# Feed-forwards with the two parts of x side by side: one 512-wide matmul for the weights' high part

## The reference

```python
h = rms_norm(x, norm_ffn_g[i])
x = x + swiglu(h, ffn_w_gate_up[i], ffn_w_down[i])      # first block
x = x + rms_norm_2(swiglu_2(h, w_gate, w_up, w_down), norm_ffn_post[layer])   # second block

def swiglu_2(h, w_gate, w_up, w_down):
    return (jax.nn.silu(h @ w_gate) * (h @ w_up)) @ w_down
```

## Time and profile before

| | us |
|---|---|
| three runs, median (range) | 2918.84 (2915.59 to 2919.42) |
| the profiled execution | 2916.95 |
| its span, first to last instruction | 2915.2 |
| TensorE busy with matmuls | 2592.3 (89%) |
| VectorE, ScalarE, GpSimd busy | 1676.4, 1193.9, 533.6 |

### The profile page before, as it was taken

How to read it: one execution, slowest core, us unless ns; L and a number is a source line. 1 busy time by engine, 2 the same in 40 slices (tenths; PEclk the granted TensorE clock), 3 DMA queues, 4 the chain that set the end, 5 groups by cost and what they waited for, 6 DMA issues and landing times. The chain is left out here.

```text
span 2915.2 us, 49758 instructions
## 1 busy us (share of the span) xinstructions
PE 2592.3 (89%) x19384; PEld 2465.6 (85%) x19390; DVE 1676.4 (58%) x2753; ACT 1193.9 (41%) x1927; POOL 533.6 (18%) x410
## 2 busy tenths in 40 slices
PE   7999898997889888999899975789988999988998
PEld 6999787997788677999799974489987999988998
DVE  3778794666555444566466675346656454334665
ACT  2534563444444323444244452234444344334443
POOL 1110692000455000000000022000002555440000
PEclk9999799999899888999899986589998999988999
DMA  4465003454334521455155532034541212103452
GB/s 158 153 207 192 16 2 112 156 182 146 99 130 155 159 33 28 143 187 189 65 173 173 167 129 73 17 116 142 182 153 58 66 59 73 66 30 116 137 183 97
DMA packets 107152, 344.26 MB, mean 118 GB/s; under 512 B 20432, under 2 KB 26160, under 8 KB 106480
## 3 DMA queue, kind: packets, MB, share of 16 engines
q1 hardware_dynamic: 106992, 342.07, 35.9%
HBM read 340.86 MB, written 1.16 MB: 117 GB/s over the span
## 5 line engine op out<-in xcount | busy, mean ns | idle before, releaser
L134 PE MATMUL ps<-h_high,hi 128*128 128x256 f32 x2936 | 851.6, 290 | 53.9 <-DVE h_low L272 38.1
L135 PE MATMUL ps<-h_low,hi 128*128 128x256 f32 x2936 | 840.6, 286 | 0.0
L136 PE MATMUL ps<-h_high,lo 128*128 128x256 f32 x2936 | 840.1, 286 | 0.0
L101 ACT ACTIVATE hi<-raw 128x1024 fp32r<-128x1024 f32 x623 | 644.7, 1052 | 439.9 <-PE ps L136 426.0
L111 DVE TENSOR_TENSOR lo<-raw,hi 128x1024 fp32r<-128x1024 f32 x521 | 629.5, 1225 | 318.7 <-ACT hi L101 318.2
L134 PEld LDWEIGHTS ps<-h_high,hi 128*128 128x128 f32 x2936 | 573.0, 195 | 62.5 <-DVE h_low L272 41.6
L135 PEld LDWEIGHTS ps<-h_low,hi 128*128 128x128 f32 x2936 | 573.2, 195 | 0.4
L136 PEld LDWEIGHTS ps<-h_high,lo 128*128 128x128 f32 x2936 | 572.9, 195 | 0.0
L111 POOL TENSOR_TENSOR lo<-raw,hi 128x1024 fp32r<-128x1024 f32 x102 | 242.6, 2383 | 491.4 <-ACT hi L101 491.3
L134 PE MATMUL ps<-hidden_h,hi 128*128 128x256 f32 x1056 | 299.3, 283 | 10.0 <-DVE lo L111 9.6
L135 PE MATMUL ps<-hidden_l,hi 128*128 128x256 f32 x1056 | 298.0, 282 | 0.0
(11 more groups left out here) (429 smaller groups left out, 4410.7 us busy)
## 6 DMA issues: line engine op xcount, KB each, us to landing
raw<-in_weights SPq DMA_DIRECT2D x623, 512.0 KB, 3.4
at_bias<-bias_group SPq DMA_DIRECT2D x64, 64.0 KB, 2.6
s_bn<-in_s_bn SPq DMA_DIRECT2D x4, 512.0 KB, 4.9
consts<-in_consts SPq DMA_DIRECT2D x1, 1794.5 KB, 9.3
x<-in_x SPq DMA_DIRECT2D x1, 1024.0 KB, 5.0
s_cT<-in_s_b SPq DMA_DIRECT2D x1, 1024.0 KB, 7.3
s_cw<-in_s_c SPq DMA_DIRECT2D x1, 1024.0 KB, 10.9
s_cT<-s_rows SPq DMA_DIRECT2D x16, 64.0 KB, 2.7
```

The source lines that it names most:

```text
L101: act.activation(k.hi[:, item % CUT, :], k.raw[:, item % RAW, :], ACT.Copy).then_inc(k.item_rounded, 1)
L134: pe.matmul(out, wh, xh, start=start, stop=False, **more)
L135: pe.matmul(out, wh, xl, start=False, stop=False, **more)
L136: return pe.matmul(out, wl, xh, start=False, stop=stop, **more)
```

## The change

Both parts of x become one tile, `both`, 128 x 2 x 8 x 256, of which `h_high` and `h_low` are views. In gate and up of every feed-forward the weight's high part multiplies both parts of x in one matmul of 512 columns into a whole bank, of which the left half takes the product with x's high part and the right half that with its low part. The weight's low part multiplies x's high part, 256 columns, into the left half. Gate and up then need a bank each: 4 and 5 for even b, 6 and 7 for odd b. ScalarE copies the right halves out, VectorE adds them to the left ones and then multiplies. As banks 6 and 7 are in use at the start, up(1) waits for the root; and layer 0's transposes go to bank 4 after down(6), with TensorE waiting for their copy. Down is as before.

```diff
+            def wide(w, bank, j):
+                wh, wl = w
+                pe.matmul(k.ps[:, bank, :], wh, k.both[:, :, j, :], start=(j == 0), stop=False)
+                return pe.matmul(k.ps[:, bank, 0:T], wl, k.both[:, 0, j, :], start=False, stop=(j == KT - 1))
 ...
                     for half in range(2):
-                        mm = product(pe, k.ps[:, 4, half * T:(half + 1) * T], w.tile(half * ITEM + j), pair_tile(src, j),
-                                     start=(j == 0 and half == 0), stop=(j == KT - 1), skip_group_check=True)
+                        mm = wide(w.tile(half * ITEM + j), 4 + half, j)
 ...
                 for half in range(2):
+                    if b == 1 and half == 1:
+                        pe.wait_ge(k.root_done.s, prep.b_root + prep.passes)
                     for j in range(KT):
-                        mm = product(pe, k.ps[:, 4 + b % 2, half * T:(half + 1) * T], w.tile((at + half) * ITEM + j),
-                                     pair_tile(src, j), start=(j == 0), stop=(j == KT - 1))
+                        mm = wide(w.tile((at + half) * ITEM + j), 4 + 2 * (b % 2) + half, j)
 ...
             # ScalarE, step b
-                act.wait_ge(k.gate_done.s, i * (2 * per) + (2 * b + b_gate + 1))
+                bank = 4 + 2 * (b % 2)
+                act.wait_ge(k.hidden_done.s, i * per + (b + b_hid - 1))
+                act.wait_ge(k.item_used, i * ROUND_ITEMS + (first + 3 * b + (2 if b == 0 else 1)))
+                act.activation(gate[:, b % 2, :], k.ps[:, bank, T:2 * T], ACT.Copy).then_inc(k.up_copied.s, 1)
+                act.wait_ge(k.item_used, i * ROUND_ITEMS + (first + 3 * b - 1))
+                act.activation(up[:, b % 2, :], k.ps[:, bank + 1, T:2 * T], ACT.Copy).then_inc(k.up_copied.s, 1)
+                act.wait_ge(k.gate_done.s, i * (4 * per) + (4 * b + b_gate + 2))
 ...
             # VectorE, step b
-                dve.tensor_tensor(gate[:, b % 2, :], k.ps[:, 4 + b % 2, 0:T], k.rs[:, 0, :], ALU.mult).then_inc(k.gate_done.s, 1)
+                dve.wait_ge(k.up_copied.s, i * (2 * per) + (2 * b + b_copied + 1))
+                dve.tensor_tensor(gate[:, b % 2, :], k.ps[:, bank, 0:T], gate[:, b % 2, :], ALU.add).then_inc(k.gate_done.s, 1)
+                dve.wait_ge(k.gate_done.s, i * (4 * per) + (4 * b + b_gate + 1))
+                dve.tensor_tensor(gate[:, b % 2, :], gate[:, b % 2, :], k.rs[:, 0, :], ALU.mult).then_inc(k.gate_done.s, 1)
 ...
-                dve.tensor_tensor(up[:, b % 2, :], k.ps[:, 4 + b % 2, T:2 * T], k.rs[:, 0, :], ALU.mult).then_inc(k.gate_done.s, 1)
-                dve.wait_ge(k.gate_done.s, i * (2 * per) + (2 * b + b_gate + 2))
+                dve.wait_ge(k.up_copied.s, i * (2 * per) + (2 * b + b_copied + 2))
+                dve.tensor_tensor(up[:, b % 2, :], k.ps[:, bank + 1, 0:T], up[:, b % 2, :], ALU.add).then_inc(k.gate_done.s, 1)
+                dve.wait_ge(k.gate_done.s, i * (4 * per) + (4 * b + b_gate + 3))
+                dve.tensor_tensor(up[:, b % 2, :], up[:, b % 2, :], k.rs[:, 0, :], ALU.mult).then_inc(k.gate_done.s, 1)
+                dve.wait_ge(k.gate_done.s, i * (4 * per) + (4 * b + b_gate + 4))
 ...
     def tensor(self, pe, b):
-        if b == 5:
+        if b == 6:
             pe.wait_ge(self.V.s, self.v0 + LAMBDA_TICK)
-            pe.transpose(self.k.ps[0:ST, 6, 0:P], self.lr, const(self.k, "ident"))
-            pe.transpose(self.k.ps[0:ST, 6, P:2 * P], self.li, const(self.k, "ident")).then_inc(self.flipped.s, 1)
+            pe.transpose(self.k.ps[0:ST, 4, 0:P], self.lr, const(self.k, "ident"))
+            pe.transpose(self.k.ps[0:ST, 4, P:2 * P], self.li, const(self.k, "ident")).then_inc(self.flipped.s, 1)
+            pe.wait_ge(self.A.s, self.a0 + 6)
 ...
-        k.hp = sb("h_high", [P, KT, T], F32R), sb("h_low", [P, KT, T], F32R)
+        k.both = sb("h_parts", [P, 2, KT, T], F32R)
+        k.hp = k.both[:, 0, :, :], k.both[:, 1, :, :]
```

More of the change, by code:

```diff
@@ L501, in swiglu @@
     rounds = (FT - 2) // per
-    b_gate, b_silu, b_hid, b_prod = k.gate_done.n, k.silu_done.n, k.hidden_done.n, k.mul_done.n
+    b_gate, b_silu, b_hid, b_prod, b_copied = k.gate_done.n, k.silu_done.n, k.hidden_done.n, k.mul_done.n, k.up_copied.n
     def walk(engine, step):
@@ L602, in step @@
                 dve.wait_ge(k.item_used, i * ROUND_ITEMS + (first + 3 * b + (2 if b == 0 else 1)))
-                dve.tensor_tensor(gate[:, b % 2, :], k.ps[:, 4 + b % 2, 0:T], k.rs[:, 0, :], ALU.mult).then_inc(k.gate_done.s, 1)
-                dve.wait_ge(k.item_used, i * ROUND_ITEMS + (first + 3 * b - 1))
-                dve.tensor_tensor(up[:, b % 2, :], k.ps[:, 4 + b % 2, T:2 * T], k.rs[:, 0, :], ALU.mult).then_inc(k.gate_done.s, 1)
-                dve.wait_ge(k.gate_done.s, i * (2 * per) + (2 * b + b_gate + 2))
+                bank = 4 + 2 * (b % 2)
+                dve.wait_ge(k.up_copied.s, i * (2 * per) + (2 * b + b_copied + 1))
+                dve.tensor_tensor(gate[:, b % 2, :], k.ps[:, bank, 0:T], gate[:, b % 2, :], ALU.add).then_inc(k.gate_done.s, 1)
+                dve.wait_ge(k.gate_done.s, i * (4 * per) + (4 * b + b_gate + 1))
+                dve.tensor_tensor(gate[:, b % 2, :], gate[:, b % 2, :], k.rs[:, 0, :], ALU.mult).then_inc(k.gate_done.s, 1)
+                dve.wait_ge(k.item_used, i * ROUND_ITEMS + (first + 3 * b - 1))
+                dve.wait_ge(k.up_copied.s, i * (2 * per) + (2 * b + b_copied + 2))
[3 more added lines that the diff above has]
+                dve.wait_ge(k.gate_done.s, i * (4 * per) + (4 * b + b_gate + 4))
                 dve.wait_ge(k.silu_done.s, i * per + (b + b_silu + 1))
@@ L626, in swiglu @@
     k.used += items
-    k.gate_done.n += 2 * FT
+    k.gate_done.n += 4 * FT
+    k.up_copied.n += 2 * FT
     k.silu_done.n += FT
@@ L824, in scalar @@
             act.wait_ge(self.flipped.s, 1)
-            act.activation(self.rows64, k.ps[0:ST, 6, 0:2 * P], ACT.Copy).then_inc(A.s, 1)
+            act.activation(self.rows64, k.ps[0:ST, 4, 0:2 * P], ACT.Copy).then_inc(A.s, 1)
     def tick(self, dve, ins):
@@ L2786, in build @@
         k.gate_done = counted("gate_and_up_scaled")
+        k.up_copied = counted("gate_and_up_low_product_copied")
         k.warm = sb("warm", [P, 1])
```

## The result

The changed kernel takes **2930.68 us** (median of 9 runs, 2925.15 to 2935.34), the kernel before beside it 2917.89 (9 runs, 2912.64 to 2922.53): ratio 1.0043 [1.0029, 1.0056], slower by 12.8 us. The prediction said 2912.2, faster or the same, with 2896 to 2926 as its range. It was wrong in sign, and the time lies outside its range.

What follows compares the result with a forecast made beforehand. TensorE, busy 89% of the span, was taken to bound the kernel. Savings of 23.0 us less costs of 16.4 gave net -6.6: 2910.3 against the profiled execution, 2912.2 us as median, with 2896 to 2926 as 8-in-10 range.

Steps and rivals of the forecast that it cites:

- The saving per tile: Gate and up: wide plus narrow matmul take 347.1 ns instead of 360, 12.9 ns saved a tile, 23.0 us in all.
- Starts: Feed-forward starts: first cut for down(0) lands 0.45 us later, 2.25 us over five loops, plus 0.5 in layer 0.
- Ends: Down(21) at five loop feed-forward ends: TensorE stalls 0.85 us each for the late hidden tile, 4.25 us in all.
- S5's rows: Layer 0, transposes moved to after down(6): rows spread and weights 4.9 us later, TensorE idle near 11.5 us.
- VectorE in layer 0: Tiles 10 to 21: added vector work makes VectorE the bound, 4.5 us more, bounds 3 and 8.
- Rival A: Wide matmul runs like the attention's `at_pl` ones: 7.7 ns a tile, 13.7 saved, 16.4 spent, +2.7: 2921.5 us; chance 0.18.
- Rival B: Wide matmul costs 240 ns, by columns' gap or two-piece operand; nothing saved: 2935.2 us; decides from 234 ns; chance 0.13.

Runs made afterwards that it cites:

- e4: Changed kernel without ScalarE's copies and VectorE's adds, all matmuls kept, x's low part computed but not added in: 2909.14 us.
- e6: Changed kernel with each gate or up item's eight wide products ahead of its eight narrow ones: wide product 230.9 ns, layers 1 to 5 feed-forwards 969.8 us.
- e1: Changed kernel with the two parts of x side by side in each feature tile, so the wide operand is one piece: 2932.55 us.
- e5: Changed kernel without the narrow product of the weights' low part in gate and up, so part of the work is left out: 229.4 ns a wide product.
- g2: g1 with set 21 of each feed-forward and sets 12 to 21 of layer 0 on the old three products, no copies or adds: 2891.66 us, ratio 0.9910.
- g1: Changed kernel with each item's eight wide products ahead of its eight narrow ones and the S5 transposes behind down(4): 2905.0 us.
- e2: Changed kernel with layer 0's transposes behind down(4) instead of down(6), their copy in ScalarE's step 4: 17.4 us less than the changed kernel.
- a_again: The changed kernel once more, unedited, for a second profile: 2931.02 us in the profiled execution.
- The pads: Runs p1, p2, q1, q2 and q3: products of zeros added ahead of the last down product of feed-forwards, as work of known price; ratios 1.0012 to 1.0053.
- p1: Kernel before with four 512-column products of zeros ahead of each feed-forward's last down product: 9.0 us over before for a price of 5.4, ratio 1.0032.
- q2: Changed kernel with eight 512-column products of zeros ahead of each feed-forward's last down product: 2934.36 us, 7.2 below its price.
- q3: e3 with four products of zeros ahead of the last down product in layers 1 to 5: 2922.38 us, 3.0 below its price.
- p2: Kernel before with eight products of zeros ahead of each feed-forward's last down product: 10.7 us over before for a price of 10.9, ratio 1.0035.
- e3: Changed kernel with wide products in layers 1 to 5 only, layer 0 and its transposes as in the kernel before: 2920.9 us.
- b1: Kernel before with only the S5 transposes moved from behind down(5) to behind down(4), their copy in ScalarE's step 4: 2905.6 us.
- q1: Changed kernel with four 512-column products of zeros ahead of each feed-forward's last down product: 2929.67 us, 6.4 below its price.

## Why the prediction was wrong

Two steps failed: the size of the saving, and the stages outside the feed-forwards, which the sum put at nothing.

**The saving per tile was about half.** I took 227.1 ns for a wide product from 512-wide products that follow one another, and measured 235.8 between narrow ones. The narrow one came at 117.1 instead of 120, together 353 for a tile (5.65 us over 16), not 347.1: 6.9 ns saved, not 12.9. Over the 1650 tiles counted for the loop feed-forwards that is 11.4 us instead of 21.3. The pitch was outside the 222 to 232 that the prediction set itself as its limit. The saving exists, with or without the copies and adds (e4). Why it is half stays open: order has a part in it (e6), the layout has none (e1), and the 5.55 us behind down(0) show the forecast pitch in the same order. By the Trainium skill, "TensorE: Matmul & The Clock Gate", section "Back-to-back issue gap", the gap of a lone 512-wide product would be 215.8 ns. Sixteen in a row without a change of width took 229.4 each here (e5), 16 above the bare 213.3 where the page's formula has 2.5.

**Starts: predicted 2.25 us slower, measured 2.1 faster.** That is the other way than the 2.25 us of the prediction's sum for them. From the first gate matmul to down(0) the five loop feed-forwards take 0.30 to 0.59 us less each: 18.43 became 18.05, 19.02 became 18.43, 18.04 became 17.74, 18.70 became 18.29 and 18.69 became 18.30. I let the table load wait for the product "as now"; but the copies bring ScalarE's table loads forward, beside the reciprocal, and that is worth more than the add costs. From the last product of zeros to down(0) it is 6.72 us in the kernel before, 6.35 after, and 6.72 again without the copies (e4).

**Ends: right.** Down(21) starts 0.89 us later at each of five ends, forecast 0.85 (the list of waits has 0.73 of it); with the slower restart the five ends cost 5.0 us, forecast 4.25. The wait is absent in e4, and g2, which does set 21 the old way, takes 193.2 for a feed-forward where g1 takes 194.0.

**S5's rows: right.** Idle 10.62 against 11.5; the two steps around the spread cost 4.3 us more, forecast 4.9. e2 removes it.

**VectorE in layer 0: right mechanism, size short.** Of the nine steps ahead of the last two downs, four take 8.77 instead of 8.50, one 9.95 and one 9.05. Against the kernel before, at 8.61 each, they cost 2.1 us, and the wait before the last down with its cold products 4.7 (1.6 of this is the clock at 0.62, which I did not price): 6.8, forecast 4.5 with 8 as its bound. Layer 0 as a whole: +10.7 (+13.3 in a_again), forecast +8.2. In mid-loop VectorE is busy 38.22 us of 50 and not 36: the 0.71 us counted distances between starts, while each of the two adds is 0.42 us of busy time. It cost nothing there.

**Outside: not in the prediction at all.** Feed-forwards: forecast -6.6, measured +2.4 (+5.3 in a_again). That alone would have given 2920 to 2923, inside the range. The rest, 6.1 us in the first profiles, 8.7 in a_again and 7.5 to 10.4 by the median, lies in stages that nobody edited and that the sum put at nothing. Their granted clock is below full (0.91 and 0.89 on average in the delta net's stage, 0.77 behind layer 3), and their cost moves when they are shifted. The two profiles cannot tell this from an effect of the change; nor could a_again. The pads show that such a move of 3 to 7 us exists (p1, q2, q3), and that the 4.5 and the 1.7 us named above also appear without wide products (p1, p2). They do not show how much of the loss it makes up, and why the kernels after, e1 and e3 lie at the dear end together was not settled.

Rival A had nearly the right saving, 7.7 ns, and its +2.7 is near the +2.4 of the feed-forwards. The second is partly luck: starts came 4.3 us better than in its sum, layer 0 and the ends worse. Rival B's deciding point, a wide matmul of 234 ns, was passed at 235.8, but neither of its mechanisms holds: e1 excludes the two pieces, and a gap that belongs to the columns would be 240 ns in every order.

## What to carry to other kernels

Price a wider matmul from one with the same neighbours, and with a margin: the same instruction took 229.4, 230.9 or 235.8 ns in three orders, and 230.4 at one place in the last of them. An exchange of matmuls for vector work pays only where the vector engines are hidden; use it in the middle of the loop and keep the old form where VectorE is the bound or where nothing is left to cover it (g2 against g1: 13 us). And a forecast of a kernel whose other stages run below full clock has an error of some us that goes with their timing and may come out alike in two profiles of one kernel. To tell it from an effect, look at the same stage in all profiles (533.7 us stood alone among sixteen), add work of a known price and see whether the sum holds beyond the spread of the medians.

## What the runs showed that was not expected

- A float32r product of 256 columns took 117.1 ns between wide ones, 118.8 in down and in groups, 120 in the old gate and up: the gap over its 106.7 bare ns is not a constant.
- ScalarE's Copy out of PSUM in the loop feed-forwards brought table loads of 1.28 us of their own: 25 of them, one for each of five rounds of five loops, beside the 28 that silu had and has. At the start it fell beside the reciprocal, and the start became shorter; in the other rounds it was hidden, with ScalarE busy 28.73 us of 50.
- The early transposes alone, on the kernel before, are worth 12 us (2918.05 on the same chip to 2905.6), as much as the change lost; 7.8 of them are in layer 0.
- The stage behind layer 3 took 327.7 to 328.0 us in after, a_again, e1, e2, e3 and p2, and 325.7 to 326.1 in before, e4, e6, p1, q2, g1 and g2; b1, q1 and q3 had 324.7, 326.9 and 323.4.
- Twelve executions of one program, e2, lie in two groups: 2908.6 to 2910.1 us at a mean granted clock of 0.917 to 0.918, and 2916.4 to 2920.9 at 0.913 to 0.915.
